# Opening of a hybrid encoder block: which memory tile is loaded and turned first, and one top-k round moved behind a weight split

## The reference, cut to what matters

```python
mem_h = rms_norm(mem, mem_norm_g[l])              # 256 x 1024
kv_m = mem_h @ w_mem_kv[l]                        # 1024 x 2048
km = rms_norm(kv_m[..., :D_MEM].reshape(B, -1, MEM_HEADS, MEM_HD), mem_k_norm_g[l])
vm = kv_m[..., D_MEM:].reshape(B, -1, MEM_HEADS, MEM_HD)
...
score = jnp.where(admissible[None], score, -jnp.inf)
_, idx = lax.top_k(score, top_k)                  # top_k = 128 of 512 keys
...
merged = (g[:, :, 0] * (y_a @ w_branch[l, 0]) + g[:, :, 1] * (y_b @ w_branch[l, 1])
          + g[:, :, 2] * (y_m @ w_branch[l, 2]))
x = x + merged @ w_out[l]
```

## Time and profile before

| | us |
|---|---|
| median of 3 runs | 954.18 |
| the profiled execution, its own time | 954.63 |
| its span in the trace | 952.7 |
| PE busy | 947.4 |
| DVE busy | 733.2 |
| ACT busy | 543.9 |
| POOL busy | 349.4 |

### The profile page before, as it was taken

One profiled execution on the slowest core, in us unless ns is written; L12 is line 12 of the kernel. 1 busy time (PEld: TensorE's weight loads), 2 busy tenths in 40 slices (PEclk: granted clock), 3 DMA queues, 4 the chain that ended last, 5 costly groups with the idle time before them and its releaser, 6 DMA issues.

```text
span 952.7 us, 13756 instructions
## 1 busy us (share of the span) xinstructions
PE 947.4 (99%) x5017; PEld 841.0 (88%) x5017; DVE 733.2 (77%) x1134; ACT 543.9 (57%) x850; POOL 349.4 (37%) x246
## 2 busy tenths in 40 slices
PE   8999999999999999999999999999999999999998
PEld 7888888888988988988988888898998989999887
DVE  6879987788996686685688566796776867984896
ACT  6876644464447546546563422585775957874341
POOL 0200834456227146145220071372613626202920
PEclk9999999999999999999999999999999999999999
DMA  8624232244532532432355324707034150538512
GB/s 285 246 89 133 79 100 59 74 133 133 158 97 67 157 109 67 144 111 78 96 201 180 131 101 156 242 21 212 1 110 122 33 155 1 177 114 301 205 44 89
DMA packets 105158, 119.31 MB, mean 125 GB/s; under 512 B 4772, under 2 KB 80136, under 8 KB 104332
## 3 DMA queue, kind: packets, MB, share of 16 engines
q1 hardware_dynamic: 105084, 118.53, 38.6%
q10 hardware_dynamic: 16, 0.00, 0.0%
HBM read 106.45 MB, written 12.07 MB: 124 GB/s over the span
## 4 chain that ended last, share of the span: by engine, by line
PE 99%; DMA 1%; SPq 0%; ACT 0%; DVE 0%; issue 0%
PE proj L833 41%; PE proj L1194 12%; PE proj L1331 9%; PE att L1352 7%; PE proj L1352 5%; PE att L1442 3%; PE proj L1390 3%; PE proj L1003 2%; PE att L1158 1%; PE att L1176 1%; PE att L1100 1%; PE att L1390 1%; PE att L1122 1%; PE att L1166 1%; PE proj L1285 1%; PE att L1146 1%
## 5 line engine op out<-in xcount | busy, mean ns | idle before, releaser
L833 PE MATMUL proj<-hT_hi,w_hi 128*128 128x512 f32 x264 | 104.1, 394 | 0.0
L833 PE MATMUL proj<-hT_hi,w_lo 128*128 128x512 f32 x264 | 103.1, 391 | 0.0
L833 PE MATMUL proj<-hT_lo,w_hi 128*128 128x512 f32 x264 | 102.9, 390 | 0.0
L2247 DVE TENSOR_TENSOR w_lo<-w_raw,w_hi 128x2048 fp32r<-128x2048 f32 x25 | 60.8, 2434 | 42.8 <-ACT w_hi L1492 40.7
L1492 ACT ACTIVATE w_hi<-w_raw 128x2048 fp32r<-128x2048 f32 x24 | 45.9, 1914 | 56.6 <-PE proj L833 55.2
L833 PE MATMUL proj<-y_hi,w_hi 128*128 128x512 f32 x192 | 75.2, 392 | 0.0
L833 PE MATMUL proj<-y_hi,w_lo 128*128 128x512 f32 x192 | 74.8, 390 | 0.0
L833 PE MATMUL proj<-y_lo,w_hi 128*128 128x512 f32 x192 | 74.7, 389 | 0.0
L3189 POOL TENSOR_TENSOR w_raw<-merged,w_raw 128x384 f32<-128x384 f32 x32 | 39.3, 1262 | 54.5 <-DVE w_lo L2598 32.4
L833 PEld LDWEIGHTS proj<-hT_hi,w_lo 128*128 128x128 f32 x264 | 49.6, 188 | 10.6
L833 PEld LDWEIGHTS proj<-hT_lo,w_hi 128*128 128x128 f32 x264 | 49.6, 188 | 9.9
(11 more groups left out here) (603 smaller groups left out, 3123.7 us busy)
## 6 DMA issues: line engine op xcount, KB each, us to landing
w_raw<-w_in_in SPq DMA_DIRECT2D x36, 512.0 KB, 4.6
w_raw<-w_in_in SPq DMA_DIRECT2D x56, 256.0 KB, 3.7
w_raw<-w_branch_in SPq DMA_DIRECT2D x12, 1024.0 KB, 5.6
merged<-w_in_in SPq DMA_DIRECT2D x38, 256.0 KB, 3.6
merged<-w_in_in SPq DMA_DIRECT2D x18, 512.0 KB, 6.0
w_raw<-w_mem_kv_in SPq DMA_DIRECT2D x10, 512.0 KB, 6.5
yF<-x_in SPq DMA_DIRECT2D x8, 512.0 KB, 10.5
w_raw<-w_in_in SPq DMA_DIRECT2D x4, 1024.0 KB, 5.1
```

What stands on the lines that cost most here:

```text
L833: ins = mm(ps, lhs[a](k, k0), rhs[b](k, k0), start=(first and k == 0 and j == 0), stop=(last and k == KH - 1 and j == 2))
L2247: V.tensor_tensor(w_lo[:, kh, :, 0:n], w_raw[:, kh, :, 0:n], w_hi[:, kh, :, 0:n].bitcast(F32), ALU.subtract).then_inc(w_lo_done, 1)
```

## The change

Four edits. SP loads half tile 1 ahead of weight piece 0. ACT and DVE take half tile 1 ahead of weight piece 1. PE turns half tile 1 before its first product, and the twelve products of the first two weight blocks are taken by weight block (both tiles with block 0, then both with block 1, its low part last). And in the first branch unit DVE does the fourth of four top-k rounds behind `b_low(3)` and no longer ahead of it.

```diff
             load_mem(0)
+            load_mem(1)
             load_piece(0, 0, 0)
-            load_mem(1)
             load_piece(1, 0, 0)
...
+            def first_part(m, k, a, b, start=False):
+                mm(banks[m][:, :], memT[a][:, k, m * P:(m + 1) * P], (w_hi, w_lo)[b][:, 0, k, :], start=start, stop=False)
+
+            turn_tile(1)
             pe.wait_ge(w_first_cast, 1)
-            first_products(0, 0, 0, 1, (half_hi, 1), (w_first_lo, 1), (half_lo, 1), weights_last=False)
-            turn_tile(1)
-            first_products(0, 0, 1, 2, (w_first_hi, 1), (w_first_lo, 2))
-            first_products(0, 1, 0, 2, (half_hi, 2), (), (half_lo, 2), weights_last=False)
+            pe.wait_ge(half_hi, 1)
+            first_part(0, 0, 0, 0, start=True)
+            pe.wait_ge(w_first_lo, 1)
+            first_part(0, 0, 0, 1)
+            pe.wait_ge(half_lo, 1)
+            first_part(0, 0, 1, 0)
+            pe.wait_ge(half_hi, 2)
+            first_part(1, 0, 0, 0, start=True)
+            first_part(1, 0, 0, 1)
+            pe.wait_ge(half_lo, 2)
+            first_part(1, 0, 1, 0)
+            pe.wait_ge(w_first_hi, 1)
+            for m in range(MT):
+                for a in range(2):
+                    first_part(m, 1, a, 0)
+            pe.wait_ge(w_first_lo, 2)
+            for m in range(MT):
+                first_part(m, 1, 0, 1)
...
             mem_high(0)
+            mem_high(1)
             piece_high(1)
-            mem_high(1)
...
             mem_low(0)
+            mem_low(1)
             piece_low(1)
-            mem_low(1)
...
-                rounds(1, 4)
+                rounds(1, 3)
                 if i:
                     b_maxes(tail)
                 b_low(n + 3)
+                rounds(1, 1)
```

## The result

| | us |
|---|---|
| before, median of 22 runs | 954.18 (953.46 to 954.74) |
| changed, median of 22 runs | 955.51 (954.72 to 957.94) |
| ratio, 95% interval | 1.0016 (1.0011 to 1.0022) |
| changed, profiled execution: its time, its span | 954.72, 952.8 |

The profiled execution of the changed kernel was the fastest of its 22, and its span is only 0.1 us above that of before. It shows both steps of the change, but with the opening at its best.

What follows compares the result with a forecast made beforehand. The prediction took PE, busy 947.4 of 952.7 us, as the bound. Opening +0.1 and moved round +1.55 summed to +1.65 us: 955.8 on the median, 956.3 on the profiled execution; range 953.8 to 956.4.

Steps and rivals of the forecast that it cites:

- What bounds the kernel: Whole kernel: PE busy 947.4 of 952.7 us, so the end moves only by what PE's idle time changes.
- The path of the opening: Opening: DVE's cast, low parts of piece 0, both half tiles, then piece 1 hold PE; twelve products done at 10.90, +0.11 us.
- the landing of weight piece 0: Opening DMA: third in SP's queue, piece 0 lands at 6.48, as half tile 1 had, so DVE's cast starts at 6.55.
- a cast before 6.2: Opening, DVE: sign that the prediction is wrong, against a first cast forecast at about 6.55.
- The moved round: First branch unit: DVE's earlier split makes POOL's fourth instruction take 2.54 instead of 0.98, delaying PE's product 3, +1.55 us.
- The prediction's other sum: First branch unit: by the skill's rule alone, POOL's fourth instruction starts when the split ends, +1.8 us, time 956.1.
- The releaser of product 3: First branch unit: ACT's first copy of `b_save` releases PE, not DVE's split; an earlier split is worth at best 0.1 us.
- Sum: Whole kernel: opening +0.1 and moved round +1.55 make +1.65 us.
- POOL going first: Rival, first branch unit: POOL's fourth instruction gets in ahead of the split, nothing lost there; 954.3 us; chance 0.25.
- The opening did gain: Rival, opening: piece 0 lands well before 6.2, gain up to 1.09; with 0.8, 954.9 or 953.4 us; chance 0.10.
- PE's clock did not fall back: Rival, opening: PE falls back from 2.4 to 1.2 GHz, losing 1.4 us; 957.2 us; chance 0.07.

Runs made afterwards that it cites:

- e7: Changed opening on PE, ACT and DVE, with SP's queue in its old order and the rounds as before: 953.75 us, ratio 0.9997.
- e1: Changed kernel with all four top-k rounds ahead of `b_low(3)` as before, so the opening alone: 953.77 us, ratio 0.9998.
- e9: Kernel before with all four top-k rounds moved behind the split `b_low(3)`: 955.33 us, ratio 1.0014.
- e2: Kernel before with only the fourth top-k round moved behind `b_low(3)`, without the changed opening: 955.42 us, ratio 1.0014.
- e6: Kernel before with the fourth round moved and DVE waiting for the end of POOL's sum before `b_low(3)`: 954.44 us, ratio 1.0003.
- e3: Kernel before with the fourth round moved and ACT's two copies of `b_save(0, 2)` ahead of `b_high(4)`: 953.82 us, ratio 0.9999.
- e5: Changed kernel whole, with ACT's copies of `b_save(0, 2)` ahead of `b_high(4)`: 953.94 us, ratio 0.9999.
- e10: Kernel before with only ACT's two copies of `b_save(0, 2)` put ahead of `b_high(4)`: 953.88 us, ratio 1.0.
- e8: Kernel before with only SP's queue changed, half tile 1 ahead of weight piece 0: 954.11 us, ratio 1.0001.

## Why the prediction was right

**What bounds the kernel** held for the steps of the change: PE's idle time accounts for the loss at product 3 in each profile. It is not all that moves the end, though: in the opening PE was also slower while busy, by up to 1.3 us in e7's profile.

**The path of the opening** held up to the sixth product: from the cast to its start it was forecast at 9.31 - 6.55 = 2.76 us and measured at 7.93 - 5.17 = 2.76. The last link did not. I had DVE's low part of piece 1 hold the last two products, by a margin of nothing (its end at 10.39, PE free for them at 10.45); in the trace that part ended 3.82 us behind the cast (forecast 3.84), and PE reached those products 4.03 behind it. The step behind the wait took 0.34 us, not 0.227. So the 4.35 us of the sum became 4.50.

**The term that was mis-sized is the landing of weight piece 0.** I put the cast at 6.55, from one landing of one execution, and it came at 5.17 to 5.88 in four profiles. The third transfer took 4.8 us from issue to landing in the profile I read, 4.1 to 4.9 in all seven profiles with the old queue, and 3.4 to 4.3 in the five with the new one; equal size and equal place did not give an equal time. The prediction named a cast before 6.2 as a sign that it is wrong, and for the opening that sign came true. The opening was forecast at +0.1 us; e1 has -0.24 on the medians. The comparison also used a single old profile whose thirteenth product, at 10.79, was the latest of six old ones. So one pair of profiles says 1.1 us gained, the means say 0.2. The total was hardly touched by this only because the gain in the medians is so small.

**The moved round** was forecast at +1.55 us by POOL's fourth instruction, and cost +1.41 (e2), with every step of the chain as forecast: 2.54 us for the instruction in the changed kernel, then ACT's rounding, its copy, and PE 0.14 behind the copy. e9 and e6 show that the meeting of the split with one POOL instruction is the cause; e3 and e5 that it reaches PE through ACT's copy. The prediction's other sum, +1.8 for an instruction that starts only when the split ends, had the split end at 244.25; it ended at 244.15 in e2. With that end and 0.98 us for the instruction it gives +1.66 (an estimate), against +1.52 in the rows, so the two sums differ less than they seemed to.

**The releaser of product 3** was ACT's copy, as read from the ends of the rows. Five profiles and e3 show it; e10 by itself does not.

**Sum.** e1 and e2 together give -0.24 + 1.41 = +1.17, measured +1.33, forecast +1.65. The difference to the forecast is the opening's 0.34 and the round's 0.14, less 0.16 that the two parts do not account for, within the intervals.

**The rivals.** POOL going first did not happen in any profile in which the two met. The opening did gain 1.1 us in the profiled execution, with the early landing that this rival named, but not in the median. PE's clock did not fall back in the changed kernel: the products behind its gaps keep their 0.23 us. But the reading behind that rival was wrong. PE was not at 2.4 GHz by 4.55: of the seven transposes in the row that begins there the first two still step by 0.21 us, and the 0.12 was a mean over both levels. In the changed kernel all seven were 0.21 apart (the row of 1.59 us), so the turns of half tile 1 began at 6.01 and not at 5.40.

## What to carry to other kernels

An instruction brought forward has to be checked against what runs beside it at its new time, not only against the one who waits for it. Where a wait has two semaphores, compare the end of both releasers with the start of the waiting instruction before moving either; here the named one had ended 0.44 us earlier. And a wait row that vanishes after an edit proves little while it also vanishes without the edit in another execution. Before a late matmul is put down to a wait, compare the step from one matmul to the next with the usual one. A difference of the order of 1 us in one profile of an opening that hangs on DMA landings is not yet a difference of the kernel: profile it again, or trust the median.

## What the runs showed of the hardware that was not expected

Beside top-k rounds (MAX8, MATCH_REPLACE8) POOL's additions kept 0.98 us each; beside DVE's subtraction of two SBUF operands one took 2.40 to 2.61, and it ended 0.87 to 0.88 us behind the subtraction in the seven cases named (0.87 to 0.90 in the others). When the subtraction began 0.25 us before the end of a POOL instruction, POOL's next one, already queued, was the one held back; DVE paid 0.1 us (1.86 against 1.76). It can pay more: in e3 a subtraction that began at 292.00, near the start of a POOL instruction (291.98 to 292.99), took 2.60 us, and POOL's next one was held behind it all the same. The first 256 KB transfers landed at times that vary by about 1 us between executions: weight piece 1, always fourth in the queue, reached ACT's rounding, which was waiting for it, at 6.60 in e8 and at 7.66 in before. PE's matmuls went from the long step to the short one at about 4.9 to 10.0 us, while the profile's granted clock read 1.00.
